# Eight sample rows on four column groups of TensorE, each with its own 128 of 512 columns

## What is computed

```
h    = rms_norm(x, norm1_g) * (1 + sc1) + sh1     # sc, sh, gt from the conditioning vector c
proj = h @ w_in                                   # 1024 x 3328: q, k, v (512 each) and 1792 more
q, k = rope(rms_norm(q)), rope(rms_norm(k))       # per head of 64
attn = dilated_attention(q, k, v)                 # samples: over cached keys and values
rw   = rwkv7_group(proj[..., 1536:])              # recurrent head group
x    = x + gt1 * (concat(attn, rw) @ w_out)       # 1024 x 1024
h2   = rms_norm(x, norm2_g) * (1 + sc2) + sh2
x    = x + gt2 * moe(h2)                          # top 4 of 32 experts, SwiGLU
```

## Time and profile before

| what | value |
|---|---|
| median of 3 runs | 2012.69 us (2010.32 to 2015.12) |
| the profiled execution | 2013.41 us, of which 2011.60 are the span |
| mean granted clock of TensorE over the span | 0.923 |
| PE, DVE, ACT busy | 1766.1, 1482.0, 1033.5 us |
| projection | about 88 to 222 us of the span |
| mix_and_route | about 654 to 776 us |

### The profile page before, as it was taken

One profiled execution on the slowest core, in us unless ns is written; L12 is line 12 of the kernel. 1 busy time (PEld: TensorE's weight loads), 2 busy tenths in 40 slices (PEclk: granted clock), 3 DMA queues, 4 the chain that ended last, 5 costly groups with the idle time before them and its releaser, 6 DMA issues. The chain is left out here.

```text
span 2011.6 us, 27868 instructions
## 1 busy us (share of the span) xinstructions
PE 1766.1 (88%) x10263; PEld 1302.1 (65%) x10263; DVE 1482.0 (74%) x1334; ACT 1033.5 (51%) x896; POOL 143.2 (7%) x144
## 2 busy tenths in 40 slices
PE   4399999965796985999999999999999999999960
PEld 0044576633684444788888888888888888887850
DVE  0165344456765445899999999999999999999955
ACT  1011222242231232677777777777777777777731
POOL 0000000001400200100000000000000000000006
PEclk8689999976798985999999999999999999999985
DMA  9831311520002318899999999999999999999736
GB/s 382 331 140 41 100 48 48 199 71 27 22 5 98 120 54 331 328 373 396 374 384 382 374 393 368 391 382 375 386 372 394 382 376 383 374 395 381 294 137 234
DMA packets 116777, 535.24 MB, mean 266 GB/s; under 512 B 14553, under 2 KB 16899, under 8 KB 82634
## 3 DMA queue, kind: packets, MB, share of 16 engines
q1 hardware_dynamic: 102512, 491.01, 62.8%
q0 software_dynamic: 7040, 25.30, 3.3%
q10 hardware_dynamic: 7162, 18.05, 2.3%
HBM read 498.42 MB, written 35.86 MB: 266 GB/s over the span
## 5 line engine op out<-in xcount | busy, mean ns | idle before, releaser
L1979 DVE TENSOR_TENSOR ex_weights_lo<-weight_ring,ex_weights_hi 128x2048 fp32r<-128x2048 f32 x256 | 574.2, 2285 | 4.3 <-ACT ex_weights_hi L1914 0.8
L1914 ACT CAST ex_weights_hi<-weight_ring 128x2048 fp32r<-128x2048 f32 x256 | 487.3, 1914 | 146.2 <-PE banks L2088 91.3
L2067 PE MATMUL banks<-ex_weights_hi,ex_rows_hi_lo 128*128 128x512 f32 x2048 | 516.9, 395 | 3.0 <-ACT ex_weights_hi L1914 3.0
L2067 PEld LDWEIGHTS banks<-ex_weights_hi,ex_rows_hi_lo 128*128 128x128 f32 x2048 | 381.5, 189 | 87.5 <-issue 6.8
L1984 DVE TENSOR_TENSOR ex_weights_lo<-weight_ring,ex_weights_hi 128x2048 fp32r<-128x2048 f32 x128 | 293.2, 2294 | 52.6 <-ACT ex_weights_hi L1921 52.5
L1921 ACT CAST ex_weights_hi<-weight_ring 128x2048 fp32r<-128x2048 f32 x128 | 244.7, 1914 | 101.2 <-PE banks L2067 101.2
L2067 PE MATMUL banks<-ex_weights_lo,ex_rows_hi_lo 128*128 128x512 f32 x1024 | 275.9, 392 | 0.0
L2088 PE MATMUL banks<-ex_weights_hi,ex_rows_hi_lo 128*128 128x512 f32 x1024 | 258.5, 395 | 2.6 <-ACT ex_weights_hi L1921 2.6
L2088 PEld LDWEIGHTS banks<-ex_weights_hi,ex_rows_hi_lo 128*128 128x128 f32 x1024 | 190.9, 189 | 54.7 <-issue 13.2
L2067 PEld LDWEIGHTS banks<-ex_weights_lo,ex_rows_hi_lo 128*128 128x128 f32 x1024 | 193.4, 189 | 41.6
L2088 PE MATMUL banks<-ex_weights_lo,ex_rows_hi_lo 128*128 128x512 f32 x512 | 136.9, 389 | 0.0
(11 more groups left out here) (342 smaller groups left out, 1721.4 us busy)
## 6 DMA issues: line engine op xcount, KB each, us to landing
weight_ring<-in_moe_w_gu SPq DMA_DIRECT2D x256, 1024.0 KB, 10.0
weight_ring<-in_moe_w_down SPq DMA_DIRECT2D x128, 1024.0 KB, 9.9
weight_ring<-in_w_ada SPq DMA_DIRECT2D x8, 3072.0 KB, 30.5
expert_rows<-ex_plain ACTq DMA_DIRECT2D x32, 512.0 KB
weight_ring<-in_w_in SPq DMA_DIRECT2D x6, 2048.0 KB, 20.9
expert_rows<-arena SPq DMA_DIRECT2D x16, 512.0 KB, 6.0
weight_ring<-in_cache_k SPq DMA_DIRECT2D x24, 256.0 KB, 3.3
weight_ring<-in_cache_v SPq DMA_DIRECT2D x24, 256.0 KB, 3.8
```

Source lines behind the costliest of these rows:

```text
L1914: nc.scalar.copy(hi_of(i), raw_chunk(m, i)).then_inc(q["gu_hi"], 1)
L1979: V.tensor_sub(lo_of(i), raw_chunk(m, i), plain(hi_of(i))).then_inc(q["gu_lo"], 1)
L2067: last = T.matmul(m.bank[n], x[:, i, :], w[:, n * 512:(n + 1) * 512], start=False, stop=(i == GU - 1 and w is lo))
```

## The change

The products of the sample tile alone are cut in four. Instead of one matmul with 512 columns into partitions 0 to 7 of a bank, there are four with 128 columns each, into partitions 32j to 32j + 7 and columns 0 to 127 of the same bank, for j = 0 to 3. The eight rows are loaded as weights for each of the four. What was one row of 512 now lies in four places, so ACT copies it with four copies of 8 x 128. For w_out the copy is new: DVE read the bank itself before, and now ACT copies both halves into the place of the result (`m.x2`) and DVE multiplies there. ACT does it in its step for tile 3, after that tile's square root and before the copies of its transposes; a new semaphore `sample_out` releases DVE.

```
@@ projection, ACT
-                nc.scalar.copy(qk_of(n, t)[0:r, :], m.bank[4 + u % 4][0:r, :]).then_inc(proj_copied, 1)
+                if t < NT:
+                    last = nc.scalar.copy(qk_of(n, t)[0:r, :], m.bank[4 + u % 4][0:r, :])
+                else:
+                    for j in range(4):
+                        last = nc.scalar.copy(qk_of(n, t)[0:r, j * P:(j + 1) * P], m.bank[4 + u % 4][32 * j:32 * j + r, 0:P])
+                last.then_inc(proj_copied, 1)
@@ projection, PE, in the loop over k
+                    for j in range(4):
+                        last = nc.tensor.matmul(m.bank[4 + u % 4][32 * j:32 * j + r, 0:P], m.ht[:, k, cols_of(t)],
+                                                w[:, k, j * P:(j + 1) * P], start=(k == 0), stop=(k == KT - 1))
@@ mix_and_route, ACT, after the square root of tile t
+                if t == NT - 1:
+                    for n in range(2):
+                        act.wait_ge(q["out_mm"], 2 * NT + n + 1)
+                        for j in range(4):
+                            last = nc.scalar.copy(m.x2[0:NB, NT, n * 512 + j * P:n * 512 + (j + 1) * P],
+                                                  m.bank[(2 * NT + n) % 4][32 * j:32 * j + NB, 0:P])
+                        last.then_inc(q["sample_out"], 1)
@@ mix_and_route, DVE, x2_tile
-                    dve.wait_ge(q["out_mm"], 2 * t + n + 1)
-                    link(V.tensor_mul(m.x2[0:r, t, c], m.bank[(2 * t + n) % 4][0:r, :], (m.gate_row if t < NT else row_s[:, 0, :])[0:r, c]))
+                    if t < NT:
+                        dve.wait_ge(q["out_mm"], 2 * t + n + 1)
+                    else:
+                        dve.wait_ge(q["sample_out"], n + 1)
+                    link(V.tensor_mul(m.x2[0:r, t, c], m.bank[(2 * t + n) % 4][0:r, :] if t < NT else m.x2[0:r, t, c], (m.gate_row if t < NT else row_s[:, 0, :])[0:r, c]))
@@ mix_and_route, PE, out_tile, in the loop over k
+                        for j in range(4):
+                            last = T.matmul(m.bank[i % 4][32 * j:32 * j + r, 0:P], m.ct[:, k, cols_of(t)],
+                                            m.w_out[n][:, k, j * P:(j + 1) * P], start=(k == 0), stop=(k == KT - 1))
```

More of the change, by code:

```diff
@@ L392, in _ @@
                 for k in range(KT):
-                    last = nc.tensor.matmul(m.bank[4 + u % 4][0:r, :], m.ht[:, k, cols_of(t)], w[:, k, :],
-                                            start=(k == 0), stop=(k == KT - 1))
+                    if t < NT:
+                        last = nc.tensor.matmul(m.bank[4 + u % 4][0:r, :], m.ht[:, k, cols_of(t)], w[:, k, :],
+                                                start=(k == 0), stop=(k == KT - 1))
+                        continue
+                    for j in range(4):
+                        last = nc.tensor.matmul(m.bank[4 + u % 4][32 * j:32 * j + r, 0:P], m.ht[:, k, cols_of(t)],
+                                                w[:, k, j * P:(j + 1) * P], start=(k == 0), stop=(k == KT - 1))
                 last.then_inc(proj_mm, 1)
@@ L1498, in mix_and_route @@
         blk_hot = a.take((NT + 1) * TOPK, BLOCKS + 1)
-        names = ("rows_in consts_in bias_in out_mm x2_done squared ms_done root_done h2_done h2_out "
+        names = ("rows_in consts_in bias_in out_mm sample_out x2_done squared ms_done root_done h2_done h2_out "
                  "h2t_psum h2t_copied logit_mm logit_read top_done exp_done chosen_done rank_mm rank_read count_mm slots_done "
@@ L1714, in out_tile @@
                     for k in range(KT):
-                        last = T.matmul(m.bank[i % 4][0:r, :], m.ct[:, k, cols_of(t)], m.w_out[n][:, k, :],
-                                        start=(k == 0), stop=(k == KT - 1))
+                        if t < NT:
+                            last = T.matmul(m.bank[i % 4][0:r, :], m.ct[:, k, cols_of(t)], m.w_out[n][:, k, :],
+                                            start=(k == 0), stop=(k == KT - 1))
+                            continue
+                        for j in range(4):
+                            last = T.matmul(m.bank[i % 4][32 * j:32 * j + r, 0:P], m.ct[:, k, cols_of(t)],
+                                            m.w_out[n][:, k, j * P:(j + 1) * P], start=(k == 0), stop=(k == KT - 1))
                     last.then_inc(q["out_mm"], 1)
```

## The result

The changed kernel takes 1995.45 us (median of 4 runs, 1991.18 to 1995.88) against 2011.51 before (4 runs, 2008.07 to 2015.12): a ratio of 0.9922, 95% interval 0.9903 to 0.9941. It is faster, by 16.1 us. The ten runs of the changed kernel together have their median at 1991.2 us.

What follows compares the result with a forecast made beforehand. PE sets the pace in the projection; in routing the wait ending last decides. Savings of 15.0 (projection) and 6.5 us (routing) sum to 21.5, giving 1991.2 us; own range 1988 to 1994, wider range 1987 to 1997.

Steps and rivals of the forecast that it cites:

- One set: Sample products: 64 short passes, four at once at 0.112 us, take 1.90 us instead of 6.97, saving 5.07.
- Projection: The q, k and v sample sets each save 5.07 us, less 0.2 for copies: 15.0 us saved.
- DVE's lag: In the projection DVE runs late behind a sample set, catches up two units later, and delays nobody.
- The copies: At the projection's end, ACT's four copies instead of one add 0.2 us (0 to 0.4).
- Routing: Routing stage, two w_out sample sets: 6.5 us saved (5.2 to 7.7).
- h2 as the next late thing: In routing, PE would wait for DVE's h2 of tile 3, so only 7.68 of 10.1 us count.
- The clock's term of 1.2 us: In routing, an earlier clock fall over tile 3's logits gives back 1.2 us, from nothing to 2.5.
- nothing else should change but the clock's chances: Stages outside projection and routing hang on barriers or requests that move along, so no further change was counted.
- the fifth rival: Sets shrink but the clock falls elsewhere, or DVE's lag holds PE: 8 to 15 us left, near 2001; 5%.
- the second rival: Sample sets' weight loads not hidden: four passes cost 0.20 us, a set 3.31 us, 1995.3 in all; 10%.
- The third: Sample sets' four groups run one after another: 7.3 us a set, 2014 us, not told from no change; 4%.
- fourth: Sample-set groups run one after another, each with its load: 12.8 us a set, about 2042 us; 3%.

Runs made afterwards that it cites:

- two groups: The changed kernel with two column groups of 256 columns and two copies in place of four of 128 and four: 1995.09 us, 0.9919.
- one place: The changed kernel with all four 128-column products on the same eight partitions, one after another, copied or read in one piece: 2014.5 us, 1.0013.
- after_again: The changed kernel itself, run again later for spread and a second profile: 1990.6 us against 2011.4 before, 0.9893, 20.8 us less.

## Why the prediction was right, and where not

**One set.** 1.90 us was forecast and 1.87 measured; the short pass costs 0.11 us for four groups, as put together from three rows of other shapes. The doubt that no row showed this form is settled by two groups (3.56) and one place (7.15).

**Projection.** 15.0 forecast, 14.8 measured. DVE's lag reached nobody, as worked out: PE's timeline has no wait from the first product to the end of v's set. The copies were mis-sized: 0.5 us more, not 0.2, as they hardly overlap (four in 1.05 us).

**Routing.** h2 as the next late thing was right, and the 7.68 us it allows were gained within 0.1 us in the first profile (7.7). The sets themselves took 5.35 us there, not the 3.8 of the sum, and PE waited 0.83 us for h2, not 2.35, because the half clock lay over the sets. The clock's term of 1.2 us was the middle of two cases: 0 there, 1.7 us over the logits in after_again.

**The step that failed** is the last of the sum, "nothing else should change but the clock's chances". The sum has nothing for attention. In all four profiles with short sets and no filler the clock was at half over its first matmuls and once more just ahead of the sample's values, 2.8 to 4.7 us together. That is the part of the fifth rival on the clock, given 5%, as an addition to the forecast and not in place of it. The first comparison shows 16.1 us where 21.5 were forecast, the second 20.8; in the first profile 14.7 + 7.7 - 4.7 + 0.3 = 18.0. Of those 4.7 the first 2.8 are in this stretch; the rest lies where kernels with and without the change differ as much (21.1 to 28.9 us in the column behind), so it is not put down to the change.

**What was luck.** The ten runs have their median at 1991.2 us, the very number forecast, though in the first profile routing did not lose its 1.2 us to the clock and attention lost what the sum did not have. The first median, 1995.45, lies outside the forecast's own range of 1988 to 1994, and inside the wider one, 1987 to 1997, which allowed for the second rival and the clock.

**The rivals.** The second, with loads not hidden, named 1995.3, and the first median was 1995.45. It is wrong all the same: the loads of a set lie within 1.65 us. The rule of the Trainium skill behind it ("TensorE: Matmul & The Clock Gate", Part 3, The mechanism) does not hold for column groups here. The third and fourth fall with the set of 1.87 us; one_place is the third made real, at 2014.5 us where 2014 was named.

**What stays open:** why the clock falls again near 380 us in the kernels with short sets and no filler, whether the short sets bring about the fall at attention's start, and what the 12 us between the fastest and slowest runs of the kernel before (2004.9 to 2016.9) are; the stages that differ from profile to profile are those in which the clock falls.

## What to carry to other kernels

Matmuls with few output rows are worth cutting over column groups when their passes are long: time falls with the number of groups, if neighbouring instructions alternate between the groups. Price what is saved by the next thing that is late (here VectorE's h2), and count the evacuation, which becomes four copies. A TensorE that stands idle in front of a barrier can start the next stage at half clock, so look at the clock behind it. With needless matmuls in that idle time attention was 3 to 5 us shorter up to the sample's values, and the 18 runs with a filler behind v's set alone have their median at 1986.7 us against the 1991.2 of the changed kernel's ten, though single runs overlap (1981.9 to 1994.3 and 1985.0 to 1995.9).

## What the runs showed of the hardware

- Column groups overlap by issue order: the same 64 passes take 1.87 us alternating and 5.81 us group after group.
- Weight loads of eight columns run under the passes of all four groups even with passes of 0.11 us: 64 loads in 1.65 us.
- Needless matmuls of either form, 1.7 to 1.9 us in front of a barrier, kept the granted clock at 1.00 behind it in five profiles of five; without them it was at half in six of eight.
- Where the clock falls decides what it costs: over attention's first matmuls (208.1 to 211.5 us) 1.4 us, over the sample sets in routing (716.7 to 720.1 us), for which nothing waited, nothing.
- ACT's small copies out of PSUM in a row hardly overlap: four of 8x128 take 1.05 us, 0.26 each.
